# Two-layer attention trunk on one core: root chains of two columns, the order of VectorE and ScalarE at five places, and 1088-byte activation rows

## What is computed

```python
for i in range(2):
    a = rmsnorm(h, norm_mix_pre[i])
    m = nsa_mixer(a, ...) if i == 0 else dilated_mixer(a, ...)
    h = h + rmsnorm(m, norm_mix_post[i])
    f = swiglu(rmsnorm(h, norm_ffn_pre[i]), ffn_w_gu[i], ffn_w_down[i])
    h = h + rmsnorm(f, norm_ffn_post[i])
# rmsnorm(x, g) = x * rsqrt(mean(x * x) + 1e-6) * g
# swiglu(h)     = (silu(h @ w_gu[:, :2816]) * (h @ w_gu[:, 2816:])) @ w_down
```

## Time and profile before

| | us |
|---|---|
| median of 3 runs | 838.91 (838.6 to 839.19) |
| the profiled run | 839.25 |
| its span | 837.5 |
| PE busy | 822.2 |
| DVE busy | 516.8 |
| ACT busy | 456.7 |
| POOL busy | 36.0 |

### The profile page before, as it was taken

One profiled execution on the slowest core, in us unless ns is written; L12 is line 12 of the kernel. 1 busy time (PEld: TensorE's weight loads), 2 busy tenths in 40 slices (PEclk: granted clock), 3 DMA queues, 4 the chain that ended last, 5 costly groups with the idle time before them and its releaser, 6 DMA issues.

```text
span 837.5 us, 11725 instructions
## 1 busy us (share of the span) xinstructions
PE 822.2 (98%) x4452; PEld 649.5 (78%) x4452; DVE 516.8 (62%) x1102; ACT 456.7 (55%) x879; POOL 36.0 (4%) x95
## 2 busy tenths in 40 slices
PE   8999999999999999999999999999999999999996
PEld 7877675778888888777877878777878888888885
DVE  5856868786545555586566565565568765555544
ACT  7846777754444344475555665555657544344431
POOL 1000005700000000000000000000000000000000
PEclk9999999999999999999999999999999999999998
DMA  9855211165664456457553536352434564456501
GB/s 333 299 192 187 89 51 52 54 220 170 213 215 161 150 197 213 159 196 266 161 192 119 174 110 202 101 201 101 155 97 155 194 216 167 151 187 215 200 1 50
DMA packets 108903, 137.49 MB, mean 164 GB/s; under 512 B 6272, under 2 KB 92336, under 8 KB 108720
## 3 DMA queue, kind: packets, MB, share of 16 engines
q1 hardware_dynamic: 107760, 132.53, 47.4%
q0 software_dynamic: 992, 4.19, 1.4%
q10 hardware_dynamic: 96, 0.02, 0.0%
HBM read 134.64 MB, written 2.10 MB: 163 GB/s over the span
## 4 chain that ended last, share of the span: by engine, by line
PE 91%; DVE 6%; ACT 2%; issue 1%; POOL 0%; ACTq 0%; POOLq 0%; DVEq 0%
PE ps L1654 81%; PE ps L1663 6%; DVE w_lo L1132 2%; PE ps L1904 1%; PE ps L1877 1%; DVE xt_lo L1164 1%; ACT xt_hi L645 1%; ACT w_hi L636 1%; PE ps L1715 0%; DVE probs L1309 0%; DVE h L1426 0%; PE ps L1916 0%; DVE h L1432 0%; ACT probs L808 0%; DVE tmp L1430 0%
## 5 line engine op out<-in xcount | busy, mean ns | idle before, releaser
L1132 DVE TENSOR_TENSOR w_lo<-w_raw,w_hi 128x1024 fp32r<-128x1024 f32 x240 | 287.8, 1223 | 94.1 <-ACT w_hi L636 91.6
L1654 PE MATMUL ps<-w_hi,xt_hi 128*128 128x512 f32 x760 | 312.1, 411 | 1.6 <-DVE w_lo L1132 1.2
L1654 PE MATMUL ps<-w_lo,xt_hi 128*128 128x512 f32 x760 | 299.7, 394 | 0.0
L1654 PE MATMUL ps<-w_hi,xt_lo 128*128 128x512 f32 x760 | 299.2, 394 | 0.0
L636 ACT ACTIVATE w_hi<-w_raw 128x1024 fp32r<-128x1024 f32 x240 | 246.4, 1059 | 0.0
L1654 PEld LDWEIGHTS ps<-w_hi,xt_hi 128*128 128x128 f32 x760 | 143.6, 189 | 38.8 <-issue 9.2
L1654 PEld LDWEIGHTS ps<-w_hi,xt_lo 128*128 128x128 f32 x760 | 143.4, 189 | 32.4
L1654 PEld LDWEIGHTS ps<-w_lo,xt_hi 128*128 128x128 f32 x760 | 144.0, 189 | 26.4
L906 ACT ACTIVATE st_hi<-ps 128x256 fp32r<-128x256 f32 x40 | 15.4, 384 | 121.3 <-PE ps L1663 121.3
L1444 DVE TENSOR_TENSOR st_lo<-ps,st_hi 128x256 fp32r<-128x256 f32 x40 | 17.0, 424 | 79.7 <-ACT st_hi L906 79.5
L1654 PE MATMUL ps<-w_hi,st_hi 128*128 128x512 f32 x160 | 63.5, 397 | 0.0
(11 more groups left out here) (234 smaller groups left out, 807.6 us busy)
## 6 DMA issues: line engine op xcount, KB each, us to landing
w_raw<-in_ffn_w_gu SPq DMA_DIRECT2D x88, 512.0 KB, 5.0
w_raw<-in_dil_w_in SPq DMA_DIRECT2D x72, 512.0 KB, 4.6
w_raw<-in_ffn_w_down SPq DMA_DIRECT2D x44, 512.0 KB, 4.5
w_raw<-in_nsa_w_in SPq DMA_DIRECT2D x20, 512.0 KB, 7.3
w_raw<-in_nsa_w_o SPq DMA_DIRECT2D x8, 512.0 KB, 4.7
w_raw<-in_dil_w_o SPq DMA_DIRECT2D x8, 512.0 KB, 4.2
w_k<-in_nsa_cmp_wk SPq DMA_DIRECT2D x2, 1024.0 KB, 7.8
w_raw<-in_nsa_cmp_wv SPq DMA_DIRECT2D x2, 1024.0 KB, 10.8
```

What stands on the lines that cost most here:

```text
L1132: dve.tensor_tensor(w_lo[:, n.slot, c:c + 1024], w_raw[:, n.slot, c:c + 1024], w_hi[:, n.slot, c:c + 1024].bitcast(F32), ALU.subtract)\
L1654: ins = pe.matmul(o, s, m, start=start, stop=stop, **kw)
```

## The change

Seven things change.

1. `XT_PITCH`: the rows of xt_hi and xt_lo are 272 columns apart instead of 258, 1088 bytes instead of 1032. To make room, the masks and the rope tables move into a zone that other tiles use at other times, and rs and rs_post become one tile.
2. DVE, NSA: `norm_nsa(3)` stands ahead of `cmp_probs(0)`, `split(12, (0,))` behind `mask_pair_nsa(5)`.
3. ACT, NSA: in `attend(14)` the second eviction p_t stands ahead of the exponentials.
4. `rsqrt_two`: at b = 1, 2 and 3 the factor of the residual for m = 1 and the factor of the next norm for m = 0 are made in one chain on two columns, from `add_post(..., next_h=b)`; the separate `h_rs` is gone. It has eleven operations (the first two fill one column each, and y * y is an operation of its own).
5. ACT at b = 1 and 3: `h_squares(b, 0)` stands ahead of `post_squares(b, 1)`.
6. DVE at b = 2: the two copies that fill the extra columns of xt stand behind the next split.
7. Dilated layer, e == 4: both halves of the split stand ahead of `dil_turn_out` on ACT, and ahead of the wait for `rs_wrapped` on DVE.

The core of the diff:

```diff
+XT_PITCH = S + 16
...
-        xt_hi = sb("xt_hi", [P, KT, S + 2], F32R)
-        xt_lo = sb("xt_lo", [P, KT, S + 2], F32R)
+        xt_hi = sb("xt_hi", [P, KT, XT_PITCH], F32R)
+        xt_lo = sb("xt_lo", [P, KT, XT_PITCH], F32R)
...
-        rs = sb("rs", [P, MT])
-        rs_post = sb("rs_post", [P, MT])
+        rs = sb("rs", [P, 2 * MT])
         ssq = sb("ssq", [P, 3 * MT])
-        nt = sb("nt", [P, 6])
+        nt = sb("nt", [P, 6, 2])
...
+                if both_turns:
+                    pt_out_nsa(turns_nsa(s - 2) + 1)
                 if s < PAIRS_NSA:
                     exp_nsa(2 * s, P * (pair_nsa(s)[1] + 1))
...
-                if s >= 2 and pair_nsa(s - 2)[1]:
+                if s >= 2 and pair_nsa(s - 2)[1] and not both_turns:
                     pt_out_nsa(turns_nsa(s - 2) + 1)
...
-            attend(14)
+            attend(14, both_turns=True)
...
+            h_squares(1, 0)
             post_squares(1, 1)
-            h_squares(1, 0)
...
+                if e == 4:
+                    split(n + k, (1,))
                 dil_turn_out(TILES[e - 1])
-                split(n + k, (1,))
+                if e > 4:
+                    split(n + k, (1,))
                 dil_attend(2 * e + 1)
...
+            def rsqrt_two(totals, of_h, dst):
+
+
+                v, y, t, y15 = (nt[:, i, :] for i in range(4))
+                dve.tensor_scalar(nt[:, 0, 1:2], of_h, D * EPS, None, ALU.add)
+                link(dve.scalar_tensor_tensor(nt[:, 0, 0:1], totals[0], D * EPS, totals[1], ALU.add, ALU.add))
+                link(dve.tensor_scalar(y.bitcast(I32), v.bitcast(I32), -0.5, RS_MAGIC, ALU.mult, ALU.add))
+                link(dve.tensor_tensor(t, y, y, ALU.mult))
+                link(dve.scalar_tensor_tensor(t, t, -0.5, v, ALU.mult, ALU.mult))
+                link(dve.scalar_tensor_tensor(y, t, RS_A, y, ALU.add, ALU.mult))
+                dve.tensor_scalar(y15, y, 1.5 * RS_K * float(D) ** 0.5, None, ALU.mult)
+                link(dve.tensor_tensor(t, y, y, ALU.mult))
+                link(dve.scalar_tensor_tensor(t, t, -0.5 * RS_K * RS_K, v, ALU.mult, ALU.mult))
...
+            norm_nsa(3)
+            cmp_probs(0)
+            mask_pair_nsa(5)
             split(12, (0,))
-            cmp_probs(0)
-            norm_nsa(3)
-            mask_pair_nsa(5)
...
+                if next_h is None:
+                    link(rsqrt(sums, rs[:, MT + m:MT + m + 1]))
+                else:
+                    dve.wait_ge(sq_h[next_h], 1)
+                    rsqrt_two(sums, ssq[:, 0:1], view(rs, 2 * MT - 1, [[1 - 2 * MT, 2]]))\
+                        .then_inc(rs_ready[next_h], 1)
+                    dve.wait_ge(rs_ready[next_h], 1)
...
-                    h_rs(2, 0)
+                gain_post(2 + 2 * layer, 1)
+                add_post(2 + 2 * layer, 1, next_h=2 if layer == 0 else None)
+                split(n0 + FFN_PIECES + 2)
+                if layer == 0:
...
-            add_post(1, 1)
+            add_post(1, 1, next_h=1)
             split(19, (1,))
-            h_rs(1, 0)
...
+                    split(n + k)
                     dve.wait_ge(rs_wrapped, 1)
```

More of the change, by code:

```diff
@@ L252, in build @@
         p_t2 = sb("p_t2", [P, 2, 512], at=at_s + 4096)
+        mask_nsa = sb("mask_nsa", [P, 2 * P], BF16, at=at_s + 9216)
+        mask_c = sb("mask_c", [P, MT, 16], at=at_s + 9728)
+        valid_c = sb("valid_c", [P, MT, 16], at=at_s + 9856)
+        cos2 = sb("cos2", [P, MT, ROT], at=at_s + 9984)
+        sin2 = sb("sin2", [P, MT, ROT], at=at_s + 10112)
         at_m = zone(2048)
@@ L671, in _ @@
             act.wait_ge(ident_ready, 1)
-            act.activation(rs_post[:, 0:1], ident[:, 0:1], ACT.Copy)
+            act.activation(rs[:, MT:MT + 1], ident[:, 0:1], ACT.Copy)
             act.wait_ge(gt_ready, 1)
@@ L829, in ot_hi_nsa, with attend @@
                    .then_inc(ot_hi[0], 1)
-            def attend(s, between=None):
+            def attend(s, between=None, both_turns=False):
                 if s >= 2:
@@ L1106, in _ @@
             xt_out(3, 0, 1, 3)
+            h_squares(3, 0)
             post_squares(3, 1)
-            h_squares(3, 0)
             split(n + 7)
@@ L1136, in rsqrt @@
             def rsqrt(totals, dst):
-                v, hv, hk, y, t, y15 = (nt[:, i:i + 1] for i in range(6))
+                v, hv, hk, y, t, y15 = (nt[:, i, 0:1] for i in range(6))
                 if len(totals) == 1:
@@ L1149, in rsqrt @@
                 link(dve.scalar_tensor_tensor(t, y, hk, y, ALU.mult, ALU.mult))
+                link(dve.scalar_tensor_tensor(t, t, 5.0 / 3.0, t, ALU.add, ALU.mult))
+                return dve.scalar_tensor_tensor(dst, t, 1.25, y15, ALU.add, ALU.mult)
+            def rsqrt_two(totals, of_h, dst):
[9 more added lines that the diff above has]
+                link(dve.scalar_tensor_tensor(t, t, -0.5 * RS_K * RS_K, v, ALU.mult, ALU.mult))
                 link(dve.scalar_tensor_tensor(t, t, 5.0 / 3.0, t, ALU.add, ALU.mult))
@@ L1419, in gain_post, with add_post @@
                 dve.tensor_tensor(tmp[:, m, 0:512], bank(2 * m), g_post[:, 0:512], ALU.mult)
-            def add_post(b, m, between=None):
+            def add_post(b, m, between=None, next_h=None):
                 dve.wait_ge(sq_post[b], 2 * m + 2)
                 total = MT + 2 * m
-                link(rsqrt([ssq[:, total:total + 1], ssq[:, total + 1:total + 2]], rs_post[:, m:m + 1]))
-                dve.scalar_tensor_tensor(h[:, m, 0:512], tmp[:, m, 0:512], rs_post[:, m:m + 1],
+                sums = [ssq[:, total:total + 1], ssq[:, total + 1:total + 2]]
+                if next_h is None:
[5 more added lines that the diff above has]
+                    dve.wait_ge(rs_ready[next_h], 1)
+                dve.scalar_tensor_tensor(h[:, m, 0:512], tmp[:, m, 0:512], rs[:, MT + m:MT + m + 1],
                                          h[:, m, 0:512], ALU.mult, ALU.add).then_inc(h_ready[b][0], 1)
@@ L1496, in ffn @@
                     dve.tensor_copy(xt_lo[:, :, S:S + 2], xt_lo[:, :, 0:2]).then_inc(xt_padded, 1)
-                gain_post(2 + 2 * layer, 1)
-                add_post(2 + 2 * layer, 1)
-                split(n0 + FFN_PIECES + 2)
             norm_nsa(15)
@@ L1604, in _ @@
                 dil_attend(2 * e, False)
-                split(n + k, (0,))
+                if e > 4:
+                    split(n + k, (0,))
                 dil_attend(2 * e, True)
                 dil_attend(2 * e + 1, False)
-                split(n + k, (1,))
+                if e > 4:
+                    split(n + k, (1,))
                 dil_attend(2 * e + 1, True)
@@ L1640, in _ @@
             gain_post(3, 1)
-            add_post(3, 1)
-            h_rs(3, 0)
+            add_post(3, 1, next_h=3)
             split(n + 7)
```

7 lines of the change are left out of this document (1 added, 6 removed).

## The result

The changed kernel takes 832.12 us (median of 4 runs, 831.95 to 832.52); the kernel before, beside it, 839.05. The ratio is 0.992 with a 95% interval of 0.9906 to 0.9933: faster, by 6.9 us. The forecast was 835.1 with a range of 833.5 to 837.4, a gain of 3.8. The direction was right, and the time fell outside the range: 3 us more were gained than the sum holds.

The account below looks back on a forecast made before the run. PE, busy 98%, was taken as the bound: an edit is worth the PE wait it removes. Gains 0 + 0.92 + 0.61 + 1.06 + 1.20 = 3.79 from 839.25 give 835.46, less 0.34: 835.1 us; range 833.5 to 837.4.

Parts of the forecast that it names:

- First place: NSA, DVE reorder of norm_nsa(3), cmp_probs(0) and a split: worth 0; rival that it pays 1.31 us: 8%.
- one wait of about 1.5: Sign for the NSA reorder on DVE: no PE wait near 92.97, but one of about 1.5 us where 99.09 stood.
- Second and third place: NSA: p_t eviction ahead of exponentials in attend(14) on ACT, gain 0.92 us; add_post chain at NSA's end, gain 0.61 us.
- Slow columns: Rival on the two-column chains: +0.54 us in each, total gain 2.94 us, so 836.0 us; chance 14%.
- Fourth place: FFN to dilated layer: gain_post and w_lo start earlier on DVE, PE's wait at 364.53 shrinks, gain 1.06 us.
- Fifth place: Dilated layer, e == 4: splits run during DVE's wait for rs_wrapped, stage_dil comes earlier, gain 1.20 us.
- Rows of 1088 bytes ... I take 0: Longer rows of xt_hi and xt_lo: no alignment shows in the weight loads, so worth 0.
- Both rivals on the pitch: xt matmuls 398 instead of 395 ns, 841.9 us, 7%; or xt weight loads 5.7 ns shorter on odd rows, 828.6 us, 3%.
- faster by the pitch: Rival: odd xt rows no longer begin mid 16-byte unit, 1140 weight loads save 6.5 us, 828.6 us; chance 3%.

Follow-up runs that it names:

- undo_first: Changed kernel with DVE's old order at the first place in NSA (norm_nsa(3), cmp_probs(0), split(12), mask_pair_nsa(5)): 832.32 us.
- alloc_only: Kernel before, with its old order and separate root chains, but the changed kernel's memory allocation (xt rows of 1088 bytes): 836.02 us.
- pitch_1024: Changed kernel with xt rows of 1024 bytes, the two copied columns left out, all other tiles in their places: 826.17 us.
- order_pad: Changed kernel with xt rows of 1032 bytes again and 896 bytes left free behind xt_lo, so later tiles keep their places: 831.12 us.
- two_pitches_258: Changed kernel, complete, with xt rows of 1024 bytes, and a second view with rows of 1032 for the dilated layer's projection: 827.71 us.
- p1024_wlo128: pitch_1024 with the w_lo ring 128 bytes further and everything behind it 256 bytes further: 834.97 us.

## Why the prediction was right and where it was wrong

**First place, worth nothing: right.** DVE's work from its last wait to the next point where PE needs it has the same length in either order, and undo_first lands at 832.32. The forecast of one wait of about 1.5 was not quite what came: 0.61 of it is taken by p_t on ACT, and the rest by probs.

**Second and third place: right**, 0.88 for 0.92 and 0.62 for 0.61. p_t starts 0.66 after its turn. The two-column chain goes from 168.65 to 170.55, 1.90 for the 1.85 of the sum; its operations take 0.15 to 0.17, and those that wait for the one before start 0.19 to 0.20 after it. "Slow columns" is refuted with it.

**Fourth place: mechanism right, size 0.15 too large.** 0.91 for 1.06: the chain was 0.05 longer and gain_post started 0.1 later than the sum took it. PE still waits for w_lo, as it was to do (360.50 is 1.12 after the turns began).

**Fifth place: right**, 1.19 for 1.20; PE came at its own time.

**"Rows of 1088 bytes ... I take 0": wrong.** This is the step that failed: the term was worth 2.9 us in the trace and 2.7 in alloc_only, in two ways that the prediction missed. It looked at the rows whose pitch changed, and not at what the longer rows push up behind them; the gain was on st and on what stands beside it (from start to start 4.4 ns less on the 480 matmuls on st, about 2 us, and 0.5 ns less on the 2280 on xt, about 1 us). And it took st as the aligned case, "whose rows lie on multiples of 1024". Measured against the weights st stood at 128 modulo 256, as badly as any. So the comparison of st (398) with xt (395) compared two misplaced tiles, and the uniform 188 ns of LDWEIGHTS said nothing, because it is 188 in pitch_1024 as well: the cost is in the gap from one matmul to the next. What was uniform in the trace of before was uniformly slow, 0.2337 us from start to start in the runs on st, where pitch_1024 has 0.2267. Both rivals on the pitch were built on the same comparison, with the mechanism in the address of one tile and not in the distance of two. The rival "faster by the pitch" had the right sign by luck: order_pad has the old rows, half of which begin in the middle of a 16-byte unit, and is no slower (831.12). The sign that the prediction named for this term, medians on xt as before within 1 ns, came true (188, and 394 for 395), and so couldn't show the failure.

**The bound.** "PE is busy for 98%, so an edit is worth the wait that it removes" was too narrow. The Trainium skill says in "Perfetto Trace Analysis", section "Identifying the Most-Contended Engine", that the matmuls' busy share is no good measure of how close a kernel is to the roofline (the best that the chip could do). The trace agrees: two_pitches_258 takes 11 us less than the kernel before with PE 98% busy in both.

**What stays open.** Why 256, and what in the chip makes the two reads hold each other up, no run here shows, nor whether the distance of one streamed tile to the next counts as well. Of a part of ACT's, DVE's and the DMAs' accesses nothing is to be seen in the runs of twelve on st in pitch_1024, whose gaps are all 0.226 or 0.227 while those engines work beside them; elsewhere it wasn't tested. What distance is best for tiles of every second column is open. The start of the program moves by up to 1.0 us between kernels that differ only in addresses, and no run was made on that.

## What to carry to other kernels

When a tile changes its size, list what moves behind it, and look at the distances of the tiles that are read at the same time, not only at each tile's own alignment. In a kernel bound by PE, compare the time from start to start of equal matmuls between stages and between kernels: a uniform pace is no proof that it is the best. And where PE waits for an engine that works without a pause between two points, only the sum of that engine's work between them counts, whatever the order.

## What the runs showed of the hardware

With stationary tiles of 128x128 whose columns lie side by side and 512 streamed columns in this 4-byte format, a matmul follows the one before after 0.2267 us if the stationary tile and the streamed ones begin at the same place modulo 256 bytes (runs on st in pitch_1024). If they don't, it is 0.233 to 0.234 in the mean, with single gaps of 0.229 to 0.238 (runs on st in before and in p1024_wlo128); 32 bytes of distance cost nearly what 64 cost. The delay is passed on to some matmuls behind. For stationary tiles of every second column the same place is not the best: 0.234 there in pitch_1024, 0.232 in the changed kernel, 0.229 with w_lo off by 128. Over the kernel this was worth 11 us together with the order: 838.8 before, 827.7 with the rows of 1024 bytes. In a chain of small operations on DVE, one that waits for the one before starts 0.19 to 0.20 us after it on two columns and mostly 0.18 to 0.20 on one, and one that doesn't 0.06 to 0.08: 1.90 us for eleven operations on two columns, 1.65 for ten on one.
